# Layer 1's first norm with full-width column sums, and all residual transposes ahead of the expert-choice list

## The chip, the cores and the metric

The kernel runs on one core of a Trainium2 chip. The metric is the device time of one execution in microseconds (us); the result of several runs is given as a median. TensorE (PE) does matmuls and transposes, ScalarE (ACT) and VectorE (DVE) read PSUM and work on SBUF, GpSimd (POOL) issues indirect DMAs and does some elementwise work, SyncE (SP) issues the weight loads. Each engine runs its own instruction stream in order, and they meet at semaphores.

## The reference, cut to what matters

One inference step of a two-layer backbone over T = 640 tokens (512 sample tokens and 128 prompt tokens), width D = 1024. Each layer is a mixer and an expert-choice mixture of experts, each behind a root-mean-square norm and followed by a gated residual:

```python
def rms_norm(x, g):
    xf = x.astype(jnp.float32)
    y = xf * lax.rsqrt(jnp.mean(xf * xf, axis=-1, keepdims=True) + RMS_EPS)
    return (y * g.astype(jnp.float32)).astype(x.dtype)

def expert_choice_ffn(h, router_w, w1, w3, w2):
    ...
    aff = jax.nn.softmax(jnp.dot(xf, router_w).astype(jnp.float32), axis=-1)
    gate, idx = lax.top_k(aff.T, cap)          # 64 sample and 16 prompt tokens for each of 16 experts
    xe = xf[idx]
    hid = jax.nn.silu(jnp.einsum('ecd,edf->ecf', xe, w1)) * jnp.einsum('ecd,edf->ecf', xe, w3)
    ye = jnp.einsum('ecf,efd->ecd', hid, w2) * gate[..., None].astype(h.dtype)
    ...

def run_layer(x, mod, l, P, rope, ctx):
    h = rms_norm(x, P['norm1_g'][l]) * (1 + scale1) + shift1     # "first norm"
    y, new = even_mixer(...) if l % 2 == 0 else odd_mixer(...)
    x = x + gate1 * y
    h = rms_norm(x, P['norm2_g'][l]) * (1 + scale2) + shift2     # "second norm"
    x = x + gate2 * expert_choice_ffn(h, ...)
    return x, new
```

## The kernel before

Activations stand turned: `xT` and `hT` hold width in 8 blocks k of 128 partitions (KD = 8) and the 640 tokens along the free axis (`seg`: 512 sample, 128 prompt). A norm needs the sum over the width, so over partitions and over the 8 blocks, for each token. All data is fp32, and each fp32 matmul is two records in the profile, each transpose one.

**Layer 1's first norm** runs while layer 0's expert output is being added. `sum_pe` (L1565 to L1585) turns the expert output block by block (L1577, five 128x128 transposes for each k, into PSUM pairs 0, 1, 2 in turn); DVE adds the gated block to `xT` (L1189 for the 512 sample tokens, L1192 for the 128 others); ACT squares it into `sq_all` (L621); and PE, three blocks behind, sums the squares over partitions (L1583): here the squares are the stationary operand and one column of ones is the moving one, so each of five matmuls for each k gives 128 sums as one column, and `acc` in PSUM pair 3 ends as 128x5. Then ACT takes the root into `root5` (L625, 128x5), DVE the reciprocal (L646) and builds five diagonal blocks `diag5` from it (L647, 128x640), PE spreads these over all partitions with ones as the stationary operand (`norm_spread_pe`, L586 and L587), ACT copies the result to `rstd` (L357, a helper line), and DVE multiplies `xT` with it block by block (L663), ACT and DVE scale and shift the blocks (L632, L655), and the first projection of layer 1 takes each block as it comes (`proj_R_pe`, L702). `keep_busy` (L343) are matmuls whose result nobody reads; 12 stand at the head of `sum_pe`, two stand before L702.

**Expert choice in layer 1** (`route_pe`, `route_act`, `route_dve`): after the router's logits PE turns the normed rows (`hr`, five token tiles, L1238), ACT copies them out and POOL stores them to DRAM as `h_rows` (L1345), DVE makes the softmax, and PE turns the affinities (L1253). DVE then searches the list of picked tokens: eight rounds of max, index and replace over 512 columns and two over 128 (L1332 to L1334). Meanwhile PE turns the residual `xT` back into rows (`residual_rows`, units `xr`, L1261, eight transposes for each of five token tiles), which the end of the kernel adds to. Tiles 0, 1, 2 stand ahead of the wait for the list (semaphore `top`), then gate and index of the list are turned (unit `gi`, L1273 and L1274), then tiles 3 and 4. ACT copies each tile to `xrow`, which has the place of the rows stored by L1345, so ACT waits for that store (`h_stored`) first. `moe_pe` follows: three `keep_busy` matmuls, the transposes of expert 0's gathered rows (L1379), two groups of 16 matmuls that lay out the gates of the residual (`grow`, L1288), and then 16 experts, the first matmuls of which are L1396. The gather of expert 0's rows is an indirect DMA that POOL issues (L1481) once DVE has copied the turned index (L1340).

**What sets the order.** PSUM is used as four pairs of banks. `take(pe, name)` gives the next pair in rotation, or the one named, and PE waits until the last unit in that pair was released by its reader; `release` and `emptied` are the other side. Code order within each engine's function is the instruction order; there is no scheduler.

Of the kernel before, what the change touches and what calls it, by code (L numbers as in the profile page):

```python
# [18 lines left out]
ACT = mybir.ActivationFunctionType  # L19
# [3 lines left out]
P = 128  # L23
D = 1024
# [54 lines left out]
def build(nc, io, outs):  # L79
    with ExitStack() as ctx:  # L80
# [5 lines left out]
        def S(name):  # L86
            if name not in sems:
                sems[name] = ctx.enter_context(nc.semaphore("s_" + name))
            return sems[name]
# [88 lines left out]
        def filled(eng, name):  # L178
            pair, n = units.of[name]
            eng.wait_ge(pair_full[pair], n)  # L180
            return PSUM[:, pair, :]

        def release(ins, name):
            ins.then_inc(pair_free[units.of[name][0]], 1)

        def emptied(eng, name):
            pair, n = units.of[name]
            eng.wait_ge(pair_free[pair], n)
# [393 lines left out]
        def norm_spread_pe(pe, l, n):  # L582
            u = ("nrb", l, n)
            ps = take(pe, u)
            pe.wait_ge(S("n_diag"), 2 * l + n + 1)
            pe.matmul(ps[:, 0:NS], ones, diag5[:, 0:NS], start=True, stop=True)  # L586
            finish(pe.matmul(ps[:, NS:T], ones, diag5[:, NS:T], start=True, stop=True), u)  # L587

        def norm_spread_act(act, l, n):
            u = ("nrb", l, n)  # L590
            release(copy(act, rstd, filled(act, u)[:, 0:T]), u)
# [19 lines left out]
        def norm_squares_act(act, l, n):  # L611
# [3 lines left out]
            for k in range(KD):  # L615
# [4 lines left out]
                    act.wait_ge(S("sq_add"), ADDS[l, n] + max(1, k - 2))  # L620
                act.activation(sq_all[:, k, :] if (l, n) == (1, 0) else sq[:, k % 2, :], xT[:, k, :], ACT.Square).then_inc(S("sq"), 1)  # L621

        def norm_root_act(act, l, n):
            ps = filled(act, ("nrm", l, n))
            release(act.activation(root5, ps[:, 0:NT], ACT.Sqrt, scale=1.0 / D, bias=1e-6), ("nrm", l, n))  # L625

        def norm_shift_act(act, l, n):
# [15 lines left out]

        def norm_rstd_dve(v, step, l, n):
            emptied(v, ("nrm", l, n))
            step(v.reciprocal(root5, root5))  # L646
            v.tensor_tensor(diag5.rearrange("p (t c) -> p t c", c=P), ident.unsqueeze(1).broadcast_to((P, NT, P)),  # L647
                            root5.unsqueeze(2).broadcast_to((P, NT, P)), ALU.mult).then_inc(S("n_diag"), 1)

        def norm_scale_dve(v, l, n):  # L650
            def shifted(k):
                normed(v, l, n, k)
                for g in range(2):
                    a, b = seg[g]
                    ins = v.tensor_scalar(hT[:, k, a:b], hT[:, k, a:b], gsc[:, l, n, k, g:g + 1],  # L655
                                          modt[:, l, 24 * n + k, g:g + 1], ALU.mult, ALU.add)
                ins.then_inc(S("h_dve"), 1)

            for k in range(KD):
                emptied(v, x_unit(l, n, k))  # L660
            emptied(v, ("nrb", l, n))
            for k in range(KD):
                v.tensor_tensor(hT[:, k, :], xT[:, k, :], rstd, ALU.mult).then_inc(S("x_dve"), 1)  # L663
                if k in H_DVE:
                    shifted(k)
# [557 lines left out]
        def route_pe(pe, l):  # L1223
# [41 lines left out]
            if l == 1:  # L1265
                pe.wait_ge(S("x_half"), 24)
                for k in range(4, KD):
                    emptied(pe, ("out", 1, k))
                residual_rows((0, 1, 2))
            pe.wait_ge(S("top"), l + 1)  # L1270
            u = ("gi", l)
            ps = take(pe, u)
            pe.transpose(ps[0:CAP, 0:16], g16, ident[0:NE, 0:NE])  # L1273
            finish(pe.transpose(ps[0:CAP, 16:32], i16f, ident[0:NE, 0:NE]), u)  # L1274
            if l == 1:
                residual_rows((3, 4))

# [286 lines left out]
        def sum_pe(pe, l):  # L1566
            un = ("nrm", 1, 0)
            acc = take(pe, un, 3)
            keep_busy(pe, acc, 12)
            for k in range(KD + 3):  # L1570
                if k < KD:
                    if k % 2 == 0:
                        pe.wait_ge(S(f"m_quarter{k // 2}"), 16)
                    u = ("ms", l, k)
                    ps = take(pe, u, k % 3)
                    for t in range(NT):
                        last = pe.transpose(ps[:, t * P:t * P + P], rows_m[:, t, k * P:k * P + P], ident)  # L1577
                    finish(last, u)
                j = k - 3
                if j >= 0:  # L1580
                    pe.wait_ge(S("sq"), 16 + j + 1)
                    for t in range(NT):
                        last = pe.matmul(acc[:, t:t + 1], sq_all[:, j, t * P:t * P + P], ones[:, 0:1],  # L1583
                                         start=(j == t == 0), stop=(j == KD - 1 and t == NT - 1))
            finish(last, un)  # L1585


# [1016 lines left out]
        def _(pe):  # L2604
            setup_pe(pe)
            for l in range(2):
# [29 lines left out]
                moe_pe(pe, l)  # L2636
                if l == 0:
                    sum_pe(pe, l)
                    norm_spread_pe(pe, 1, 0)

        @block.scalar
        def _(act):
            step = Steps(act, S("act_step"))
            setup_act(act, step)
            for l in range(2):
# [3 lines left out]
                norm_root_act(act, l, 0)  # L2649
                if l == 0:  # L2650
                    mod_act(act, 2)
                norm_spread_act(act, l, 0)
                if l == 0:
                    mod_act(act, 3)
                norm_shift_act(act, l, 0)
                if l == 0:
# [158 lines left out]
```

## Time and profile before

| | us |
|---|---|
| median of 3 runs | 1795.73 |
| lowest and highest | 1794.01, 1798.09 |
| the profiled execution, its own time | 1794.16 |
| its span, first to last instruction | 1791.7 |
| PE busy | 1607.9 (90%) |
| DVE, ACT, POOL busy | 633.5, 439.5, 239.3 |
| granted TensorE clock, mean of the span | 0.953 |

A granted clock of 1.00 is 2.4 GHz, one of 0.50 is 1.2 GHz. A timeline row gives start, length, engine, line, what is written and read, the count, and in brackets the idle time of the engine before it with what ended it. PE is a matmul's stream and PEld a weight load, which overlaps it. The chain of waits is followed back from the last instruction: at each step to what released it.

### The profile page before, as it was taken

To read this page: it belongs to the slowest core of one execution; us is meant where nothing else is said; L and a number is where in the kernel's file an instruction comes from. 1 tells how busy PE (TensorE), PEld (TensorE's weight loads), DVE (VectorE), ACT (ScalarE), POOL (GpSimd) and SP (SyncE) were. 2 spreads that over 40 slices of the span, in tenths; PEclk is the share of its full clock that TensorE was granted. 3 is DMA by queue.
4 is the path that set the end of the run, shared out by engine and by line. 5 is a ranking of instruction groups with operands and counts; after the bars stand their busy time and mean duration, and the time that the engine had idled before them with its cause. 6 is when DMAs were issued, how large, how long until landed. Compare 5 with 4: busy or idle time off the path is not lost.

```text
span 1791.7 us, 37993 instructions
## 1 busy us (share of the span) xinstructions
PE 1607.9 (90%) x16758; PEld 1040.3 (58%) x16758; DVE 633.5 (35%) x1290; ACT 439.5 (25%) x734; POOL 239.3 (13%) x237
## 2 busy tenths in 40 slices
PE   5999976999959999999999989888899959999992
PEld 2554434664527677676555558666675536776761
DVE  4234466652260000003129646645462270000003
ACT  3211175551031111102110246432231031111110
POOL 0000000000001111100000026156440000111113
PEclk8999997999969999998999999999899979999996
DMA  9932281244218999994121100011115227999994
GB/s 341 307 115 94 100 288 46 95 142 188 94 74 307 385 382 394 380 379 143 47 71 71 50 1 1 1 50 50 49 50 200 73 85 247 372 388 387 386 394 142
DMA packets 90319, 330.09 MB, mean 184 GB/s; under 512 B 10708, under 2 KB 16456, under 8 KB 82024
## 3 DMA queue, kind: packets, MB, share of 16 engines
q1 hardware_dynamic: 76016, 287.29, 42.1%
q0 software_dynamic: 9168, 32.65, 6.6%
q10 hardware_dynamic: 5032, 8.65, 1.3%
q8 instruction: 80, 1.31, 0.3%
q14 instruction: 23, 0.19, 0.0%
HBM read 303.79 MB, written 24.78 MB: 183 GB/s over the span
## 4 chain that ended last, share of the span: by engine, by line
PE 83%; DVE 9%; ACT 3%; issue 2%; DMA 2%; POOL 0%; ACTq 0%; DVEq 0%
PE pairs L223 27%; PE pairs L1396 16%; PE pairs L1408 12%; PE pairs L1379 2%; PE pairs L343 2%; PE pairs L1096 2%; PE pairs L1110 1%; PE pairs L1886 1%; PE pairs L1866 1%; PE pairs L2093 1%; PE pairs L1849 1%; PE pairs L490 1%; PE pairs L461 1%; PE pairs L2104 1%; PE pairs L702 1%
## 5 line engine op out<-in xcount | busy, mean ns | idle before, releaser
L223 PE MATMUL pairs<-hT,ring 128*128 128x128 f32 (+1 forms) x1120 | 306.2, 436 | 2.2 <-ACT hT L357 2.2
L223 PEld LDWEIGHTS pairs<-hT,ring 128*128 128x128 f32 x1120 | 170.3, 192 | 139.0 <-issue 139.0
L357 ACT ACTIVATE arena<-pairs 128x512 f32<-128x512 f32 (+6 forms) x212 | 123.7, 602 | 430.3 <-PE pairs L223 198.8
L223 PE MATMUL pairs<-ring,hT 128*128 128x512 f32 (+1 forms) x448 | 177.4, 557 | 0.0
L1396 PEld LDWEIGHTS pairs<-arena,ring 128*64 128x64 f32 x4096 | 142.9, 137 | 13.6 <-issue 13.6
L1396 PEld LDWEIGHTS pairs<-arena 128*64 128x64 f32 x4096 | 142.8, 137 | 13.2 <-issue 13.1
L1396 PE MATMUL pairs<-arena 128*64 128x80 f32 x4096 | 145.5, 233 | 1.6 <-ACT arena L1431 1.0
L1396 PE MATMUL pairs<-arena,ring 128*64 128x80 f32 x4096 | 145.8, 233 | 0.5 <-issue 0.5
L223 PEld LDWEIGHTS pairs<-ring,hT 128*128 128x128 f32 x448 | 84.8, 190 | 92.1 <-issue 89.1
L1464 DVE TENSOR_SCALAR hT<-pairs,arena 80x512 f32<-80x512 f32 x32 | 23.9, 747 | 272.0 <-ACT hT L1440 272.0
L1408 PE MATMUL pairs<-ring,arena 128*80 128x512 f32 x256 | 112.7, 593 | 0.2 <-DMA ring<-in_exp_w 0.2
L1408 PE MATMUL pairs<-arena 128*80 128x512 f32 x256 | 112.5, 592 | 0.0
L1460 DVE TENSOR_TENSOR arena<-hT,pairs 128x160 f32<-128x160 f32 x64 | 20.5, 321 | 249.3 <-PE pairs L1396 249.3
L357 DVE COPY arena<-pairs 128x512 f32<-128x512 f32 (+7 forms) x37 | 25.2, 703 | 185.1 <-PE pairs L223 178.7
L1491 POOL DMA_INDIRECT moe_rows<-hT,arena x32 | 45.4, 1420 | 293.7 <-DVE hT L1464 293.7
L1408 PEld LDWEIGHTS pairs<-ring,arena 128*80 128x80 f32 x256 | 37.7, 152 | 63.1 <-issue 62.9
L1408 PEld LDWEIGHTS pairs<-arena 128*80 128x80 f32 x256 | 37.8, 153 | 62.6 <-issue 62.6
L1440 ACT ACTIVATE hT<-pairs,arena 80x512 f32<-80x512 f32 x32 | 21.9, 683 | 212.1 <-PE pairs L1408 212.1
L1431 ACT ACTIVATE arena<-pairs 128x640 f32<-128x640 f32 x32 | 22.5, 703 | 185.6 <-PE pairs L1379 185.6
L1189 DVE SCALAR_TENSOR_TENSOR xT<-pairs,modt,xT 128x512 f32<-128x512 f32 x24 | 18.0, 750 | 140.8 <-PE pairs L223 125.7
L343 PE MATMUL pairs<-cst 128*128 128x512 f32 x118 | 63.4, 680 | 3.8 <-ACT arena L357 2.1
L1481 POOL DMA_INDIRECT hT<-h_rows,arena x32 | 29.4, 917 | 241.3 <-PE pairs L1379 199.5
(393 smaller groups left out, 2139.6 us busy)
## 6 DMA issues: line engine op xcount, KB each, us to landing
arena<-in_exp_w SPq DMA_DIRECT2D x48, 2048.0 KB, 18.8
ring<-in_exp_w SPq DMA_DIRECT2D x48, 2048.0 KB, 20.1
ring<-in_w_mod SPq DMA_DIRECT2D x24, 2048.0 KB, 8.2
ring<-in_w_in_ab SPq DMA_DIRECT2D x5, 2048.0 KB, 11.9
ring<-in_w_in_cd SPq DMA_DIRECT2D x5, 2048.0 KB, 7.8
ring<-in_w_out SPq DMA_DIRECT2D x4, 2048.0 KB, 8.8
moe_rows<-arena POOLq DMA_DIRECT2D x2, 2560.0 KB, 12.8
h_rows<-arena POOLq DMA_DIRECT2D x2, 2560.0 KB, 8.2
```

Source lines behind the costliest of these rows:

```text
L223: last = pe.matmul(out, lhs(k), rhs(k), start=(k == 0), stop=(k == KD - 1))
L343: pe.matmul(ps[:, 0:512], ident, cst[:, 0:4, :].rearrange("p a b -> p (a b)"), start=True, stop=True)
L357: return eng.activation(dst, src, ACT.Copy) if eng is nc.scalar else eng.tensor_copy(dst, src)
L1096: pe.matmul(ps[:, 0:512], q, k[:, 0:512], start=True, stop=True)
L1379: last = pe.transpose(ps[:, o:o + CAP], xe[par][:, k::KD], ident[0:CAP, 0:CAP])
L1396: last = pe.matmul(lin_of(j, f)[c:c + 64, :], w[:, k, f * P + c:f * P + c + 64], rhs, start=(k == 0), stop=(k == KD - 1))
L1408: last = pe.matmul(PSUM[0:CAP, 3, 512 * half:512 * half + 512], hid[par][:, f, :], w2[:, f, 512 * half:512 * half + 512], start=(f == 0), ...
L1431: act.activation(xeT[par], ps, ACT.Copy).then_inc(pair_free[0], 1)
L1440: act.activation(ye[par][:, 0:512], PSUM[0:CAP, 3, 0:512], ACT.Copy, scale=gateT[:, bass.ds(i, 1)])\
L1464: v.tensor_scalar(ye[par][:, 512:1024], PSUM[0:CAP, 3, 512:1024], gateT[:, bass.ds(i, 1)], None, ALU.mult).then_inc(pair_free[3], 1)
L1481: g.indirect_dma_start(xe[e % 2], None, DR["h", l], off(e)).then_inc(S(f"gathered{e % 2}"), 16)
L1491: g.indirect_dma_start(DR["m", l], off(e), ye[e % 2], None, compute_op=ALU.add)\
```

## The change

Three things are edited.

1. In `sum_pe` the sums of layer 1's first norm take `ones` (128x128) as the stationary operand and the squares as the moving one, in two matmuls for each k (512 and 128 columns): each gives the sums of all its tokens on every partition, and `acc` is 128x640.
2. ACT takes the root over 128x640 from PSUM straight into `rstd`, DVE the reciprocal of it in place, and `diag5`, the two spreading matmuls, their PSUM unit (`nrb`) and ACT's copy go for this norm alone. The other three norms are as before; the counts of `n_diag` are renumbered.
3. In `route_pe` of layer 1 `residual_rows` for all five tiles stands ahead of the wait for `top`.

```diff
@@ norm_spread_pe
-            pe.wait_ge(S("n_diag"), 2 * l + n + 1)
+            pe.wait_ge(S("n_diag"), (1, 2, 0, 3)[2 * l + n])
@@ norm_root_act
             ps = filled(act, ("nrm", l, n))
+            if (l, n) == (1, 0):
+                release(act.activation(rstd, ps[:, 0:T], ACT.Sqrt, scale=1.0 / D, bias=1e-6), ("nrm", l, n))
+                return
@@ norm_rstd_dve
             emptied(v, ("nrm", l, n))
+            if (l, n) == (1, 0):
+                step(v.reciprocal(rstd, rstd))
+                return
@@ norm_scale_dve
-            emptied(v, ("nrb", l, n))
+            if (l, n) != (1, 0):
+                emptied(v, ("nrb", l, n))
@@ route_pe
-                residual_rows((0, 1, 2))
+                residual_rows(range(NT))
             pe.wait_ge(S("top"), l + 1)
             ...
-            if l == 1:
-                residual_rows((3, 4))
@@ sum_pe
-                    for t in range(NT):
-                        last = pe.matmul(acc[:, t:t + 1], sq_all[:, j, t * P:t * P + P], ones[:, 0:1],
-                                         start=(j == t == 0), stop=(j == KD - 1 and t == NT - 1))
+                    for a, b in seg:
+                        last = pe.matmul(acc[:, a:b], ones, sq_all[:, j, a:b], start=(j == 0), stop=(j == KD - 1))
@@ block.tensor
                     sum_pe(pe, l)
-                    norm_spread_pe(pe, 1, 0)
@@ block.scalar
-                norm_spread_act(act, l, 0)
                 if l == 0:
+                    norm_spread_act(act, l, 0)
                     mod_act(act, 3)
```

On PE, at the end of `sum_pe`, before (L1577 are the turned expert blocks, L1583 the sums, L586 and L587 the spreading, L702 the projection):

```order
L1577 MATMUL pairs<-cst,arena 128x128 x5
L1583 MATMUL pairs<-cst,arena 128x1 x20
L586 MATMUL pairs<-arena,cst 128x512
L587 MATMUL pairs<-arena,cst 128x128
L343 MATMUL pairs<-cst 128x512 x2
L702 MATMUL pairs<-ring,hT 128x512 x16
```

The same place after (all lines are some numbers on: L1583 are now the turned blocks, L1589 the sums, L710 the projection; the four pairs of L1589 are the last four blocks' sums):

```order
L1583 MATMUL pairs<-cst,arena 128x128 x5
L1589 MATMUL pairs<-arena,cst 128x512
L1589 MATMUL pairs<-arena,cst 128x128
L1589 MATMUL pairs<-arena,cst 128x512
L1589 MATMUL pairs<-arena,cst 128x128
L1589 MATMUL pairs<-arena,cst 128x512
L1589 MATMUL pairs<-arena,cst 128x128
L1589 MATMUL pairs<-arena,cst 128x512
L1589 MATMUL pairs<-arena,cst 128x128
L343 MATMUL pairs<-cst 128x512 x2
L710 MATMUL pairs<-ring,hT 128x512 x16
```

No PE instruction stands any more between the last sum and the two `keep_busy` matmuls.

On PE around the list of picked tokens in layer 1, with the semaphores that each instruction waits for, before (L1261 residual rows, L1273 and L1274 the turned list, L343 `keep_busy`, L1379 expert 0's rows):

```order
L1261 MATMUL pairs<-cst,xT 128x128 [waits s_pair_free1]
L1261 MATMUL pairs<-cst,xT 128x128 x7
L1273 MATMUL pairs<-cst,arena 80x16 [waits s_pair_free2,s_top]
L1274 MATMUL pairs<-cst,arena 80x16
L1261 MATMUL pairs<-cst,xT 128x128 [waits s_pair_free3]
L1261 MATMUL pairs<-cst,xT 128x128 x7
L1261 MATMUL pairs<-cst,xT 128x128 x7
L1261 MATMUL pairs<-cst,xT 128x128 [waits s_pair_free0]
L1261 MATMUL pairs<-cst,xT 128x128 x7
L343 MATMUL pairs<-cst 128x512 [waits s_pair_free3,s_pair_free0,s_pair_free2,s_pair_free1]
L343 MATMUL pairs<-cst 128x512 x2
L1379 MATMUL pairs<-cst,hT 128x80 [waits s_pair_free0,s_gathered0]
```

And after (L1269 residual rows, L1281 and L1282 the turned list, L1385 expert 0's rows):

```order
L1269 MATMUL pairs<-cst,xT 128x128 [waits s_pair_free1]
L1269 MATMUL pairs<-cst,xT 128x128 x7
L1269 MATMUL pairs<-cst,xT 128x128 [waits s_pair_free2]
L1269 MATMUL pairs<-cst,xT 128x128 x7
L1281 MATMUL pairs<-cst,arena 80x16 [waits s_pair_free3,s_top]
L1282 MATMUL pairs<-cst,arena 80x16
L343 MATMUL pairs<-cst 128x512 [waits s_pair_free0]
L343 MATMUL pairs<-cst 128x512 x2
L1385 MATMUL pairs<-cst,hT 128x80 [waits s_pair_free0,s_gathered0]
```

All 40 residual transposes stand ahead of the list's wait, and the pairs that these instructions take are one lower in the rotation, since the unit `nrb` is gone.

## Rows read from the trace of the kernel before

**Rows 1.** The page: the chain of waits by engine, shares of the span.
```profile
PE 83%; DVE 9%; ACT 3%; issue 2%; DMA 2%; POOL 0%; ACTq 0%; DVEq 0%
```
**Rows 2.** Chain of waits, 824 to 849 us: start, length, engine and line.
```profile
825.85 1.01 PE pairs L1583 x10
826.86 0.60 PE pairs L1577 x5
...
833.28 8.34 PE pairs L1583 x40
```
**Rows 3.** Windows of PE, 822 to 854 us: length, busy, granted clock, DMA, GB/s.
```profile
826.00:830.00 4.00, 4.00 (x39) 1.00 0.47 129
830.00:832.00 2.00, 2.00 (x17) 0.78 1.06 378
844.00:848.00 4.00, 4.00 (x8) 0.50 0.00 0
848.00:850.00 2.00, 2.00 (x6) 0.95 0.01 4
```
**Rows 4.** Chain of waits around 1441 us: matmuls of 512 and 128 moving columns.
```profile
1440.80 0.87 PE pairs L1231 x2
1441.67 0.22 PE pairs L1232 x2
```
**Rows 5.** Timeline, 841 to 849 us: from the last sum to the projection.
```profile
841.64 0.17 ACT L625 ACTIVATE sm<-pairs 128x5 f32<-128x5 f32 x1 [5.24 <-PE pairs L1583]
843.11 2.04 PE L586 MATMUL pairs<-arena,cst 128*128 128x512 f32 x2 [1.50 <-DVE arena L647]
845.62 0.70 ACT L357 ACTIVATE arena<-pairs 128x640 f32<-128x640 f32 x1 [3.80 <-PE pairs L587]
846.45 3.77 DVE L663 TENSOR_TENSOR hT<-xT,arena 128x640 f32<-128x640 f32 x5 [3.49 <-ACT arena L357]
848.57 3.70 PE L702 MATMUL pairs<-ring,hT 128*128 128x512 f32 x8
```
**Rows 6.** Groups by form on DVE: reciprocals by width, count, busy, mean ns.
```profile
L2388 DVE RECIPROCAL sm<-sm 128x40 f32<-128x40 f32 x1 | 0.4, 403 | 0.8 <-ACT sm L2268 0.8
L1055 DVE RECIPROCAL sm<-sm 128x16 f32<-128x16 f32 x1 | 0.2, 243 | 0.0
L646 DVE RECIPROCAL sm<-sm 128x5 f32<-128x5 f32 x4 | 0.8, 188 | 13.2 <-ACT sm L625 13.2
```
**Rows 7.** Windows of PE, 1452 to 1484 us: length, busy, granted clock, DMA, GB/s.
```profile
1456.00:1462.00 6.00, 0.00 (x0) 0.77 0.96 397
1483.00:1484.00 1.00, 1.00 (x4) 0.96 0.00 0
```
**Rows 8.** Timeline, 1462 to 1480 us: copies of residual rows, the list, the gather.
```profile
1462.20 2.86 ACT L357 ACTIVATE arena<-pairs 128x1024 f32<-128x1024 f32 x3 [8.83 <-DMA h_rows<-arena]
1474.44 0.24 PE L1273 MATMUL pairs<-cst,arena 16*80 16x16 f32 x1 [19.09 <-DVE arena L1336]
1475.45 0.98 POOL L1481 DMA_INDIRECT hT<-h_rows,arena  x1 [20.60 <-DVE arena L1340]
1479.56 4.55 PE L343 MATMUL pairs<-cst 128*128 128x512 f32 x6 [1.21 <-ACT arena L357]
```
**Rows 9.** Chain of waits, 1474 to 1498 us.
```profile
1474.75 3.62 PE pairs L1261 x16
...
1484.12 0.84 PE pairs L1379 x8
...
1488.58 9.00 PE pairs L1396 x256
```
**Rows 10.** One line's DMAs: issue to landing of gathers (L1481), then of stores (L1345).
```profile
DMA to landing us min/median/max: 3.8/3.9/4.0
DMA to landing us min/median/max: 8.2/8.2/8.2
```
**Rows 11.** What PE waited for, 1488 us to the end: in total, times, longest.
```profile
PE pairs L1408 <- DMA ring<-in_exp_w: 0.2, 1, 0.2
```

## The prediction

> **What bounds the kernel now.** I read the chain first, then the two places that the diff touches. The page gives 83% of the chain to PE [rows 1], so what shortens a stretch where the chain runs through PE or waits for it shortens the run. Both places are on that chain. At the first norm of layer 1 it runs through PE's turns of the expert output and the column sums, alternating [rows 2], then ACT, DVE, PE, ACT, DVE, ACT in turn, until the projection starts at 848.57 [rows 5]. At the expert choice it runs through DVE's search of the list, then the turned list on PE (1474.44) [rows 8], and from there only through PE: residual tiles 3 and 4, `keep_busy`, expert 0's rows, the gates, the experts [rows 9]. Behind both places PE sets the pace: in the whole stretch from 1488 us on it waited 0.2 us for anything but itself [rows 11], and the weight loads wait for PE's release of their slots, so they start earlier along with it. A gain at either place should reach the end whole.
>
> **The clock at the first norm is the thing to see.** The granted clock is 1.00 until about 830, while one-column sums and transposes are all that PE does, then it falls to 0.50 in the window 830 to 832 and comes back at about 848.2 (0.95 over 848 to 850) [rows 3]. So the last four blocks' sums ran at half speed: 8.34 us for four [rows 2], 2.09 each, against 1.01 for one at full clock.
>
> **Part 1a, the sums.** A full-width sum is one matmul of 512 and one of 128 moving columns. At clock 1.00 such matmuls took 0.87 and 0.22 [rows 4], 1.09 together, against 1.01 for five one-column ones [rows 2]: at equal clock the new form costs 8 x 0.08 = 0.6 us more. But PE streams columns nearly without a pause in it (1.09 of each 1.09 + 0.60), as it does in stretches where the clock stayed 1.00, where before 1.01 of 1.61 were weight loads with one column each. I take it that the clock stays at 1.00. From the first sum at 825.85 there are 8 x 1.09 + 4 x 0.60 = 11.1 us of work, ending at 836.97 instead of 833.28 + 8.34 = 841.62: **-4.65**. Nothing else is late there: the last block's transposes are done at 825.85 + 4 x 1.69 = 832.6, and its sum can't start before 835.9, which leaves 3.3 us for DVE's add and ACT's square of 640 elements, operations of a size that takes 0.70 to 0.75 [rows 5].
>
> **Part 1b, from the last sum to the blocks.** Before, 841.62 to 846.45, which is 4.83 us of root, reciprocal, diagonal, spreading and copy. After: a root over 128x640 out of PSUM, near the copy of the same size, 0.70 [rows 5], 0.1 for the hand-over, and a reciprocal of 640 elements. The trace has none wider than 40: 5 elements took 0.188, 16 took 0.243, 40 took 0.403 [rows 6]. The slope is 6.1 ns an element from 5 to 40 and 6.7 from 16 to 40, so 0.403 + 600 x 6.1 or 6.7 gives 4.1 to 4.4; I take 4.2. With 0.05 of hand-overs: 5.05, so **+0.2**. The wide reciprocal eats all that the removed steps give.
>
> **Part 1c, PE's idle time behind it.** PE now goes from the last sum into two `keep_busy` matmuls, 2 x 0.87 = 1.7 us, to 838.7, and then has nothing until the first block is scaled and shifted: 836.97 + 5.05 + 2.12 (846.45 to 848.57, rows 5) = 844.1. Before, spreading and `keep_busy` filled the time up to L702, and the clock was up as it began. In an idle stretch that began 19.09 us ahead of 1474.44, so at 1455.35 [rows 8], the clock fell at about 1459.2 (0.77 over 1456 to 1462) [rows 7], 3.9 us in. 5.4 us of idle time is longer, so I expect the projection to start at 0.50. It came back 5.1 us after work resumed at 843.11 [rows 3, 5] and 3.5 us after 1479.56 (0.96 over 1483 to 1484) [rows 7, 8]. Half of that is lost: 1.75 to 2.55, nothing if the clock doesn't fall; **+1.8**. The blocks themselves don't bound it: DVE gives one each 0.75, and ACT's part kept up with a PE at full clock before (8 records, two blocks, in 3.70) [rows 5].
>
> Sum of part 1: -4.65 + 0.2 + 1.8 = **-2.65**.
>
> **Part 2, the residual tiles.** Tiles 3 and 4 leave the chain: 3.62 from 1474.75, and 1.2 of waiting for ACT to copy them ahead of `keep_busy` at 1479.56 [rows 8, 9]. Now `keep_busy` starts at 1474.75. It is still at half clock, since PE had been idle: 3 matmuls x 2 x 0.87 = 5.2 us, where before they took 4.55 because the clock came back within them. That ends at 1479.95. Expert 0's rows then have to be there: the gather was issued at 1475.45 and gathers landed in 3.8 to 4.0 [rows 8, 10], 1479.35, so hidden by 0.6. L1379 starts at 1479.95 instead of 1484.12: **-4.2**. It and the gates take 1488.58 - 1484.12 = 4.46, as before, if the clock is back by then, 5.2 us after work resumed. Bounds: -4.8, where the gather is the limit; -3.3, if the clock is 1.7 us late. The moved instructions are free where they go: PE was idle for 19 us. One new wait comes with it: tile 4 takes the pair of tile 0, which ACT copies only once the store of `h_rows` has landed, and the turned list is queued behind tile 4 on PE. ACT's copies began at 1462.20 [rows 8], so tile 4 is turned by about 1464.5, some 10 us before the list. ACT copies five tiles in place of three inside DVE's search and has nothing to do there.
>
> The rotation is one pair off through layer 1. The reuse distance stays four, and I cost it at nothing, within 0.5 either way.
>
> **The sum:** -2.65 - 4.2 = -6.85 against the profiled execution's 1794.16, giving 1787.3. That execution lies 1.57 under the median of the three; against the median it is 1795.73 - 6.85 = **1788.9**.
>
> **A rule that would make it otherwise.** Were the reciprocal eight passes over its elements, it would cost eight times a plain 128x640 multiply (3.77 for five, 0.754 each, rows 5): 6.0 us, so +1.8 on the sum, 1790.7. The 40-element row is 0.403 where eight passes at 0.754/640 an element would make 0.377 and leave next to nothing fixed, while the 5-element row shows some 0.15 fixed. So the trace leans to the slope, yet doesn't exclude it. The Trainium skill, in "VectorE: DVE Perf Modes", section "First, the fixed hardware budget", says that the reciprocal is an iterated divide with a repeat count of 8.
>
> **The rivals.** (A) The clock falls in the sums all the same, as before. Part 1a is then nothing, the sum is +0.2 + 1.8 - 4.2 = -2.2: 1793.5. For it: transposes are 0.60 of each round and were in the stretch that lost the clock. Against: the column sums now stream. (B) Eight passes, 1790.7, as above. (C) The clock survives the idle time: -8.65, 1787.1. Against it is the fall after 3.9 us. (D) Slower: PE is stuck in tile 4. The list is turned only after the store of `h_rows` has landed and two tiles are copied. The price is one us for each us that the store lands after about 1472; from 1472 + 6.85 = 1479 on, 17 us later than here, the kernel is slower than before, and at 1484 the time is 1800.7. The store landed at 1462.2. Part 2 then only trades its gain away. (E) The change does nothing on the chain, because something late elsewhere holds the end: 1795.7; rows 11 speak against it.
>
> **How the numbers follow.** Forecast 0.55, A 0.15, B 0.15, C 0.08, D 0.03, E 0.04. A change of 0.2% is 3.6 us, about what a measurement can tell from none: under 1792.1 is faster. The forecast, B and C are, but for some scatter (three runs of before span 4.1 us): 0.77. A and E are within 0.2%, with that scatter 0.19; slower 0.04. The range reaches from C with the best bound of part 2 (1786) less 0.5, to A: 1785.5 to 1793.5.
>
> **What would show it.** In the profile after: granted clock 1.00 through the sums, last sum about 4.7 us earlier (part 1a); one reciprocal of 4.1 to 4.4 us (1b; 6.0 would be B); PE idle for some 5.4 us ahead of the projection and 0.50 in its first 3 to 5 us (1c); no PE record between the turned list and `keep_busy`, and expert 0's rows about 5.2 us after the list, not 9.4 (part 2). Wrong would be: the clock down in the sums, a gather that lands after `keep_busy`, or PE waiting for weights among the experts.

## The result, and the profile after

| | before | after |
|---|---|---|
| median, us | 1796.72 (4 runs, 1794.01 to 1798.09) | 1784.80 (4 runs, 1783.37 to 1789.75) |
| ratio after / before | | 0.994, 95% interval 0.9916 to 0.9964 |
| the profiled execution, its own time | 1794.16 | 1789.75 |
| its span | 1791.7 | 1787.8 |

The kernel is faster, by 11.9 us in the medians. I had predicted 6.85 us. The predicted ratio, 1788.9 / 1795.73 = 0.9962, lies in the interval of the measured one, near its slow end. The predicted range ended at 1785.5, and the median is 0.7 us below it. A second series of the same kernel (e1 below) gave 1785.14, ratio 0.9937. So the direction was right and the size was too small. The profiled execution of after was the slowest of its four, and that of before was quicker than most of its kind. The two traces show 3.9 us of difference between them; the medians show three times that.

The page of after, with busy times by engine and the chain by engine (of before: rows 1):

```profile
span 1787.8 us, 37877 instructions
PE 1604.2 (90%) x16706; PEld 1031.6 (58%) x16706; DVE 637.9 (36%) x1289; ACT 439.7 (25%) x733; POOL 239.1 (13%) x237
PE 83%; DVE 10%; ACT 3%; DMA 2%; issue 2%; POOL 0%; ACTq 0%; DVEq 0%
```

PE is still 83% of the chain. DVE's rounded share reads 10% instead of 9%; the 4.16 us of the reciprocal are now on the chain in one piece.

**Part 1, the norm.** PE in windows from 830 to 854 us: length, busy, granted clock, DMA share, GB/s. In rows 3 the clock of before is 0.78 in the first of these.

```profile
830.00:832.00 2.00, 2.00 (x13) 1.00 0.46 71
832.00:836.00 4.00, 4.00 (x21) 1.00 1.07 393
836.00:840.00 4.00, 4.00 (x15) 1.00 1.02 375
840.00:844.00 4.00, 0.30 (x1) 1.00 0.03 7
844.00:848.00 4.00, 2.28 (x3) 0.55 0.00 0
...
850.00:854.00 4.00, 4.00 (x9) 0.85 0.00 0
```

The chain of waits of after in this stretch: start, length, engine and line. L1583 are the turned blocks, L1589 the wide sums, L627 the root, L651 the reciprocal, L671 and L636 scale a block, L710 is the projection (of before: rows 2).

```profile
827.75 1.08 PE pairs L1589 x4
828.83 0.55 PE pairs L1583 x5
...
834.26 4.34 PE pairs L1589 x16
...
838.62 0.71 ACT arena L627
...
839.43 4.16 DVE arena L651
...
843.61 0.83 DVE hT L671
...
844.47 1.21 ACT hT L636 x2
...
845.72 16.72 PE pairs L710 x32
```

The timeline of after at its two important rows (of before: rows 5):

```profile
839.43 4.15 DVE L651 RECIPROCAL arena<-arena 128x640 f32<-128x640 f32 x1 [4.12 <-ACT arena L627]
845.72 4.63 PE L710 MATMUL pairs<-ring,hT 128*128 128x512 f32 x5 [5.42 <-ACT hT L636]
```

The clock stays at 1.00, which is 2.4 GHz, through all sums, and the last four blocks take 4.34 us where they took 8.34. One round is 1.08 + 0.55. The reciprocal is 4.15 us. PE is idle for 5.42 us ahead of the projection. The clock goes to 0.50 (1.2 GHz) in the window 844 to 848, shortly before the idle time ends, and comes back in the window 850 to 854. So the projection's 32 records take 16.72 us; before they took 13.91, with the clock up.

**Part 2, the list.** The chain of after from the turned list (L1281) to the experts (L1402), and two timeline rows: ACT's copies of the five residual tiles, PE's turns of the last one, and the wait of expert 0's rows for their gather (of before: rows 8 and 9).

```profile
1474.74 0.24 PE pairs L1281
...
1475.05 4.89 PE pairs L343 x6
1479.94 0.97 PE pairs L1385 x8
1480.91 3.61 PE pairs L1294 x32
1484.53 9.00 PE pairs L1402 x256
```

```profile
1462.51 4.69 ACT L357 ACTIVATE arena<-pairs 128x1024 f32<-128x1024 f32 x5 [8.83 <-DMA h_rows<-arena]
1463.58 1.97 PE L1269 MATMUL pairs<-cst,xT 128*128 128x128 f32 x8 [7.06 <-ACT arena L357]
1479.80 0.30 PEld L1385 LDWEIGHTS pairs<-cst,hT 80*128 80x128 f32 x2 [0.90 <-DMA hT<-h_rows,arena]
```

From the turned list to the experts' first matmul it is 1484.53 - 1474.74 = 9.8 us; before it was 1488.58 - 1474.44 = 14.1. The last tile is turned by 1465.5, some 9 us before the list. The gather is only just hidden: the weight load at 1479.80 had waited for it.

### The profile page after: what moved, and what is told of

It reads as the page before. It is cut to its first block, busy times and chain, and to the rows that moved or that the text cites. A ratio compares the mean times of both kernels' runs of the same rounds, so it can differ in the third digit from the quotient of the medians.

```text
span 1787.8 us, 37877 instructions
## 1 busy us (share of the span) xinstructions
PE 1604.2 (90%) x16706; PEld 1031.6 (58%) x16706; DVE 637.9 (36%) x1289; ACT 439.7 (25%) x733; POOL 239.1 (13%) x237
## 3 DMA queue, kind: packets, MB, share of 16 engines
q10 hardware_dynamic: 5032, 8.65, 1.3%
## 4 chain that ended last, share of the span: by engine, by line
PE 83%; DVE 10%; ACT 3%; DMA 2%; issue 2%; POOL 0%; ACTq 0%; DVEq 0%
PE pairs L223 27%; PE pairs L1402 16%; PE pairs L1414 12%; PE pairs L1385 2%; PE pairs L1104 2%; PE pairs L343 1%; PE pairs L1118 1%; PE pairs L1871 1%; PE pairs L1891 1%; PE pairs L2098 1%; PE pairs L1854 1%; PE pairs L710 1%; PE pairs L490 1%; PE pairs L461 1%; PE pairs L2109 1%
## 5 line engine op out<-in xcount | busy, mean ns | idle before, releaser
L1402 PEld LDWEIGHTS pairs<-arena,ring 128*64 128x64 f32 x4096 | 142.8, 137 | 14.5 <-issue 14.5
L1402 PEld LDWEIGHTS pairs<-arena 128*64 128x64 f32 x4096 | 142.7, 137 | 13.1 <-issue 13.0
L1402 PE MATMUL pairs<-arena,ring 128*64 128x80 f32 x4096 | 145.7, 233 | 1.5 <-issue 1.5
L1402 PE MATMUL pairs<-arena 128*64 128x80 f32 x4096 | 145.4, 233 | 1.5 <-ACT arena L1437 1.0
L1414 PEld LDWEIGHTS pairs<-ring,arena 128*80 128x80 f32 x256 | 37.7, 152 | 62.8 <-issue 62.6
L343 PE MATMUL pairs<-cst 128*128 128x512 f32 x118 | 60.8, 656 | 2.6 <-DVE hT L1470 1.7
```

Source lines behind the costliest of these rows:

```text
L343: pe.matmul(ps[:, 0:512], ident, cst[:, 0:4, :].rearrange("p a b -> p (a b)"), start=True, stop=True)
L1402: last = pe.matmul(lin_of(j, f)[c:c + 64, :], w[:, k, f * P + c:f * P + c + 64], rhs, start=(k == 0), stop=(k == KD - 1))
L1414: last = pe.matmul(PSUM[0:CAP, 3, 512 * half:512 * half + 512], hid[par][:, f, :], w2[:, f, 512 * half:512 * half + 512], start=(f == 0), ...
```

## Experiments

What had to be explained was that the medians differ by more than the two traces. The suspects were: the clock in the sums (my theory), the pair rotation, one part hiding more than its trace showed, and the profile of before being an unusual one. Kernels that were measured together share their runs of before: median 1795.57 for e1 to e4 and 1796.31 for e5 to e8 (17 runs each), 1796.0 for e9 to e12 (11 runs). The three groups ran on different chips, so a kernel of one group is compared with one of another by its ratio to before. A bracket behind a ratio is its 95% interval.

### e1: the changed kernel again

> The changed kernel as it is, with more runs on one chip together with its two halves. Theory 1 (the sum of the prediction): about 6.4 to 6.9 us under the kernel before, and the 11.9 us between the two medians of four runs is partly scatter. Theory 2 (something outside the two places gives 4 to 5 us more, for example the PSUM pairs that are one lower through all of layer 1): 10 to 12 us under it again.

1785.14 us (5 runs, 1782.79 to 1787.32), ratio 0.9937 [0.9922, 0.9953]. The gain is 10.4 us in the medians. The larger value was no accident of the first series.

### e2: the norm alone

```diff
-                residual_rows(range(NT))
+                residual_rows((0, 1, 2))
             pe.wait_ge(S("top"), l + 1)
             ...
+            if l == 1:
+                residual_rows((3, 4))
```

> Only the norm's part of the change (wide sums, root and reciprocal; the shifted pairs come with it), residual tiles 3 and 4 behind the list as before. Theory 1: -2.0 to -2.7 us: the sums end 4.7 us earlier for the clock, the wide root and reciprocal give back 0.2, the projection's start at 1.2 GHz 1.8 to 2.8. Theory 2: -6 to -8 us, since the shifted pairs belong to this half. In its profile expert 0's first matmuls stand about 14 us behind the turned list, as in the kernel before.

1785.61 us (5 runs), ratio 0.9947 [0.9931, 0.9962]: the norm alone is worth 10.0 us in the medians, 9.5 by the ratio. I had given it 2.65, and neither theory had as much. Its trace also shows what the residual tiles cost in that state. The chain from the first of tiles 3 and 4 (L1269) on:

```profile
1468.49 3.60 PE pairs L1269 x16
1472.10 3.27 PE pairs L343 x6
1475.36 0.84 PE pairs L1387 x8
```

The `keep_busy` matmuls took 3.27 us, where before they took 4.55, since the clock came back within them (0.66 in the window 1472 to 1474). And they did not have to wait for ACT's copy of tile 4, which starts only as they do:

```profile
1472.13 1.02 ACT L357 ACTIVATE arena<-pairs 128x1024 f32<-128x1024 f32 x1 [0.68 <-PE pairs L1269]
```

That is the pair rotation at work. In before tile 4 takes pair 0, the one that `keep_busy` needs next; one pair lower it takes pair 3. From list to experts it is 11.6 us here, against 14.1 in before with the same order of code: 1.3 us of the difference are the clock, 1.2 the wait for the copy. Against the mean of three executions of before, this one is 3.5 us shorter at the norm and its records, 2.9 from the list on, and 5.4 between DeltaNet and the second norm, which the edit doesn't touch (table below).

### e3: the residual tiles alone

The edits of the norm undone, that of `residual_rows` kept.

> Only the residual tiles moved ahead of the list's wait, the norm as before. Theory 1: -4.2 us (bounds -3.3 to -4.8), all of it between the turned list and expert 0's first matmuls: 9.6 us there in place of 14.1, and nothing elsewhere. Theory 2: also about -4. If the two halves add up to e1, nothing lies in their combination.

1792.95 us (11 runs, 1790.56 to 1795.56), ratio 0.9986 [0.9975, 0.9996]: 2.6 us in the medians, where I had predicted 4.2. Its chain behind the list:

```profile
1480.04 5.41 PE pairs L343 x6
1485.45 0.84 PE pairs L1377 x8
...
1489.91 6.09 PE pairs L1394 x171
```

From the list at 1479.17 to the experts it is 10.7 us in this execution. `keep_busy` begins 0.87 us behind the list, and not 0.31 as in after: with the old rotation the turned list lies in pair 0, and DVE has to copy it out first. The 10.7 us are 3.4 to 3.9 less than the 14.1, 14.2 and 14.6 of three profiles of before, and the upper end of the median's gain (0.9975, 4.5 us) holds it. The two parts together (2.6 + 10.0) are 12.6, the whole 10.4 to 11.9: they add up within the intervals.

### e4: eight `keep_busy` matmuls in PE's idle time

```diff
-                    keep_busy(pe, ps, 2)
+                    keep_busy(pe, ps, 8)
```

> The changed kernel with 8 instead of 2 of the matmuls that nobody reads ahead of layer 1's first projection: 7.0 us at full clock from the last sum on, which ends about when the first block is there (7.2 us). Theory 1: the clock stays at 2.4 GHz into the projection, whose first 32 records take 13.9 us instead of 16.7, so -1.8 to -2.8 us against the changed kernel. A rival (the loss lies in the first blocks' arrival, not in the clock): no change, and the same 16.7 us.

1783.66 us (6 runs, 1780.14 to 1788.3), ratio 0.9931 [0.9913, 0.995]. PE in the window behind the reciprocal, and the chain at the projection:

```profile
844.00:848.00 4.00, 3.73 (x10) 1.00 0.00 0
```

```profile
845.13 14.00 PE pairs L710 x32
```

With PE occupied, the clock stays at 1.00 and the 32 records take 14.00 us, as in before. So the idle time, and nothing else in the change, was what made them 16.7 and 16.0 (after and e1). That settles part 1c: its cost is 2.0 to 2.8 us. In the medians e4 is 1.5 us under e1, inside the intervals.

### e5: the pair rotation as before

```diff
                     sum_pe(pe, l)
+                    units.next += 1
```

> The changed kernel with the rotation of the PSUM pairs moved on by one behind the column sums, so that every later unit of layer 1 has the pair that it had in the kernel before. The norm alone gave 9.5 us in medians where its place in the traces gives 2 to 5. Theory 2 (the pairs, one lower, give the rest): 4 to 6 us slower than the changed kernel. Theory 1 and theory 3 (the old form costs more than the one profile shows, because how early the clock falls in it is a matter of luck): no change against it, about 0.9937 of the kernel before.

1788.27 us (6 runs, 1781.5 to 1790.94), ratio 0.9944 [0.9921, 0.9966]. With the rotation of before and the rest of the change, the gain stands. Theory 2 had this kernel 4 to 6 us slower than the changed one. By the ratios it is 1.3 us slower than e1, and its interval reaches 4 us to each side, so the medians alone would allow the rotation a share. The trace shows one effect of it (list at 1473.87):

```profile
1474.73 4.88 PE pairs L343 x6
```

`keep_busy` starts 0.86 us behind the list where after has 0.31, as in e3. So the lower rotation is worth some 0.55 us in the changed kernel. No stretch of e5's trace is longer than in both traces of the changed kernel by more than 0.9 us (table below).

### e6 and e11: the old sums with wide matmuls between them

Before, with one 128x512 matmul that nobody reads behind each of the first seven blocks' sums (e6), and with two (e11). The sums themselves remain 128x5.

```diff
                         last = pe.matmul(acc[:, t:t + 1], sq_all[:, j, t * P:t * P + P], ones[:, 0:1],
                                          start=(j == t == 0), stop=(j == KD - 1 and t == NT - 1))
+                    if j < KD - 1:
+                        keep_busy(pe, acc[:, 512:1024], 1)      # 2 in e11
```

> The kernel before (one-column sums, narrow root and reciprocal, spreading) with one 128x512 matmul that nobody reads behind each of the first seven blocks' sums: 6.1 us more work for PE at 2.4 GHz, in the stretch that sets the time. Theory 1 (a PE that streams no columns loses the clock): the clock stays at 2.4 GHz until the sums end, the spreading is at full clock too, and the projection starts 24.5 to 25.5 us after the first turned block, against 25.7 in the profile of the kernel before and 28.0 in that of the run with the tiles alone: 0 to -3 us. Theory 3: -2 us or more, since the unlucky cases go. If columns had nothing to do with the clock: +6 to +12 us.

1799.04 us (12 runs, 1793.47 to 1806.41), ratio 1.0018 [1.0001, 1.0035]. This expectation missed: the kernel is some 3 us slower than before and not up to 3 us faster, and the clock fell ahead of the end of the sums. The profiled execution is the second slowest of the twelve (1806.34 us).

> e6 with two unread 128x512 matmuls behind each of seven blocks' sums instead of one: 12.2 us more work for PE than the kernel before. In e6 the clock lasted until about 841, 10 to 13 us longer than without, and then fell with one matmul for each five one-column sums. Theory 1 (streamed columns hold the clock): 1.00 until the last sum at about 849, so that from the first turned block to the projection's start there are 30 to 31.5 us. If the one-column sums are what drops it whatever stands between them: a fall ahead of 845 and 35 us or more.

1795.97 us (one run). In the chain of e6 the sums are 1.01 us until 840 and 1.92 after it; the window is below them:

```profile
839.39 1.01 PE pairs L1583 x10
840.40 1.86 PE pairs L343 x2
842.26 1.92 PE pairs L1583 x10
```

```profile
840.00:844.00 4.00, 4.00 (x16) 0.54 0.01 5
```

In e11 the last sum is at full clock too:

```profile
849.27 1.02 PE pairs L1583 x10
```

So what PE does between the one-column sums decides when the clock falls: at 828 to 832 with none (four executions), at 840 with one wide matmul to each block, and not within the sums with two (one execution each). All three stretches have PE busy throughout. That is what the change rests on, shown without the change. The extra work costs more than it gives: from the first turned block to the projection e6 takes 30.7 us and e11 32.1, before 25.7 to 28.0, after 20.9. Replacing narrow sums by wide ones gives the columns for nothing.

### e7 and e10: the kernel before, profiled again

> The kernel before, profiled once more. Theory 3: the stretch from the first turned block to the end of the first projection's 32 records differs from that of the first profile (39.7 us) and is nearer to that of the run with the tiles alone (42.0) or over it; with the new form it was 37.0 to 37.6 three times. Theory 1 without luck: 39.7 again, within 0.3.

1797.43 us (one run, span 1795.5).

> The kernel before, profiled a third time. If the norm's stretch is mostly the longer one: from the first turned block to the projection's start 28.0 us again, not 25.7, and a fall of the clock near 1128 us, between the grouped attention and DeltaNet, as in all three profiles with narrow sums so far and in none with wide ones.

1798.32 us (one run, span 1795.8). In e7 the fall comes three us earlier than in rows 3. Its windows and its chain:

```profile
826.00:830.00 4.00, 4.00 (x30) 0.75 0.50 142
830.00:832.00 2.00, 2.00 (x12) 0.50 1.08 391
```

```profile
827.83 0.90 PE pairs L1577 x5
828.73 1.92 PE pairs L1583 x10
```

Two more rounds run at 1.2 GHz. From the first turned block to the projection it is 28.0 us here and in e3, 25.7 and 25.8 in before and e10. So theory 3 had e7 right, and the expectation of e10 missed: the longer stretch is not the usual one. Its second part, a fall of the clock near 1128 us, held. The profile that I predicted from was one of the quicker kind: against a mean of 26.5 over the three executions of before, it made this stretch 0.8 us too short.

### e9: the projection later, with the clock up

Ten `keep_busy` matmuls in e4's place of eight.

> e4 with 10 in place of 8 unread matmuls ahead of the projection: at full clock everything behind it comes 1.5 us later (8.7 us of work in a 7.2 us gap), and nothing else changes. What is open is why the kernels with narrow sums took 282 to 288 us in layer 1's second half (from DeltaNet's first transposes to the second norm's root) where those with wide sums took 279 to 282.5. Theory 3 (when the later stages come, not what they do, sets how often the clock falls in them): the medians differ by something other than 1.5 us, and the profile has other falls of the clock than e4 behind 1040 us. Theory 4 (the later stages don't depend on it): +1.5 us against e4, that is 0.994 of the kernel before.

1784.96 us (6 runs, 1782.11 to 1789.95), ratio 0.9948 [0.9931, 0.9964]. The stretch up to the projection is 22.2 us where e4 has 20.9: +1.3. The medians differ by the same 1.3, the ratios by 3 us, each uncertain by as much. In the profiled execution, though, the later stages were 4 us shorter than in e4's (278.5 against 282.5 from DeltaNet to the second norm). So a shift of 1.3 us can go with another pattern of falls later. The medians don't show it as a rule.

### e8 and e12: the gates' rows ahead of the list as well

e4, and besides in layer 1 the gates' 16 matmuls (`grow`) stand ahead of the list's wait. In e8 five `keep_busy` matmuls stand behind the list, in e12 three. ACT's copies of the gates' rows move ahead along with them. (The 16 matmuls are two groups of eight, each group 16 records.)

```diff
                 residual_rows(range(NT))
+                gate_rows_pe(pe)
             pe.wait_ge(S("top"), l + 1)
...
-            keep_busy(pe, PSUM[:, 0, :], 3)
+            keep_busy(pe, PSUM[:, 0, :], 5 if l else 3)
```

> The changed kernel with 8 matmuls ahead of the projection as in e4, and the 32 gate records (L1294) turned ahead of the list too, while DVE searches it, with 5 instead of 3 of the unread matmuls behind the list in layer 1. Expected: expert 0's rows at the gather's landing, some 4.9 us after the turned list as before, its first matmuls 6.5 to 7 us after the list in place of 9.7; -3 us against e4, -4.5 to -5.5 against the changed kernel. A rival: the clock is down again behind the list (PE was waiting), and half of the gain goes.

1782.42 us (6 runs, 1778.49 to 1786.01), ratio 0.992 [0.99, 0.9941].

> e8 with 3 instead of 5 unread matmuls behind the list. In e8 the clock was at 1.2 GHz behind the list, the five took 7.6 us and held expert 0's rows until 1475.0 where the gather had landed at about 1472. Expected: 5.2 us at half clock, so the rows at 5.2 us and the first expert matmuls at 7.1 us behind the list in place of 9.6; -2.4 us against e8 for that. A rival: the experts' first matmuls then run at half clock for some us and the gain halves.

1784.32 us (6 runs, 1778.64 to 1790.51), ratio 0.9938 [0.9917, 0.9958]. The chain of e8 and then of e12 behind the list:

```profile
1467.45 7.55 PE pairs L343 x10
1474.99 0.86 PE pairs L1387 x8
...
1476.81 9.07 PE pairs L1404 x256
```

```profile
1472.08 4.02 DMA hT<-h_rows,arena
...
1476.14 1.13 PE pairs L1387 x8
...
1478.23 10.71 PE pairs L1404 x256
```

In e8 the five `keep_busy` matmuls ran mostly at half clock and took 7.55 us. From list to experts it is 9.7 us, no better than the 9.8 of after, where 6.5 to 7 had been expected; the rival of that expectation, a clock that is down behind the list, is what came. In e12 it is 7.1 us, as expected, and the gather now sets it (4.02 us on the chain). But the experts' first 256 records take 10.71 us instead of 9.00, with the clock at 0.50 in this window:

```profile
1480.00:1482.00 2.00, 2.00 (x35) 0.50 0.26 88
```

One more such trade: here work taken off PE ahead of the experts was paid in clock within them, and instead of 2.4 us less the median is 1.9 us more than e8's. e8 has the lowest median of all. Its interval overlaps those of e4 and e12, so what is shown is that e8 beats before, not that it beats e4 or the changed kernel. The gates' move has no gain of its own that these runs show.

## Why the prediction was right, and too small

The table shows the stretches of all fourteen profiled executions in us, each cut at the same instructions: first turned block of the expert output, first projection matmul, last of its 32 records, first transposes of DeltaNet, root of the second norm, turned list of layer 1. The last column is the span. Before, e7 and e10 are the same kernel, and so are after and e1.

| | to first block | to projection | its 32 records | to DeltaNet | to second norm | to list | to end | span |
|---|---|---|---|---|---|---|---|---|
| before | 822.9 | 25.7 | 14.0 | 288.4 | 282.0 | 41.4 | 317.3 | 1791.7 |
| e7 | 822.2 | 28.0 | 14.0 | 287.2 | 285.3 | 41.3 | 317.5 | 1795.5 |
| e10 | 823.7 | 25.8 | 14.0 | 288.4 | 284.9 | 40.9 | 318.1 | 1795.8 |
| e3, tiles | 824.1 | 28.0 | 14.0 | 287.2 | 284.9 | 41.0 | 313.0 | 1792.2 |
| e2, norm | 823.7 | 21.0 | 16.0 | 287.5 | 278.7 | 41.3 | 314.7 | 1782.9 |
| after | 824.8 | 20.9 | 16.7 | 288.4 | 282.4 | 41.5 | 313.1 | 1787.8 |
| e1, after | 824.0 | 20.9 | 16.0 | 287.6 | 282.1 | 41.2 | 313.6 | 1785.4 |
| e4 | 824.2 | 20.9 | 14.0 | 287.5 | 282.5 | 41.7 | 313.2 | 1784.0 |
| e9 | 824.3 | 22.2 | 14.0 | 286.9 | 278.5 | 41.4 | 312.8 | 1780.1 |
| e8 | 825.1 | 20.9 | 14.0 | 286.2 | 280.3 | 40.6 | 312.6 | 1779.7 |
| e12 | 824.3 | 21.0 | 14.0 | 287.5 | 282.6 | 41.7 | 312.6 | 1783.7 |
| e5 | 825.0 | 21.0 | 16.4 | 289.3 | 280.8 | 41.4 | 313.7 | 1787.6 |
| e6 | 824.3 | 30.7 | 14.0 | 289.3 | 287.9 | 41.9 | 315.9 | 1804.0 |
| e11 | 824.3 | 32.1 | 13.9 | 288.5 | 278.3 | 40.8 | 316.1 | 1794.0 |

**Part 1a, the sums: right, and 0.25 us larger.** Clock 1.00 throughout. From the first sum to the last it is 838.60 - 827.75 = 10.85 us, predicted 11.1, since a round was 1.63 and not 1.69. Before it was 15.77. So 4.9 us instead of 4.65 against that profile, and 0.8 us more against the mean of before's three. Rival A is out: in all eight executions with wide sums the clock stayed at 1.00 until the last of them, though the transposes, 0.55 of each 1.63 us, are still there. e6 and e11 point the same way. Whether the transposes had a share in the fall before, beside the one-column sums, these runs don't separate.

**Part 1b, root and reciprocal: right.** 838.60 to 843.61 is 5.01 us, predicted 5.05. The reciprocal took 4.15 us; the slope of its narrow forms had given 4.1 to 4.4, with 4.2 taken. Rival B, eight passes or 6.0 us, is out. The Trainium skill ("VectorE: DVE Perf Modes", section "First, the fixed hardware budget") gives the reciprocal a repeat count of 8. The measured 4.15 us is 5.5 times the 0.754 of a plain multiply of this size, so the repeat count can't be read as eight times the time.

**Part 1c, the idle time: right in kind, too small.** 5.42 us idle, predicted 5.4, and the projection starts at 0.50. The 32 records cost 2.8 us more in after and 2.0 in e1, predicted 1.8 with bounds of 1.75 to 2.55. That half of the time until the clock is back is lost was right: in after it was back at 851.2 (0.89 in the window 851 to 852), 5.5 us after the projection began, for a cost of 2.8, and in e1 at 849.0, 4.1 us after, for 2.0. What was mis-sized is that time. The prediction had 3.5 to 5.1 us and took +1.8, nearly the low end, without a reason. And the 3.5 was read too short: it counts from 1479.56, but PE had been at work on the list and tiles 3 and 4 from 1474.44 to 1478.35, so the clock came back 8.6 us after work had resumed there. The fall comes earlier in e1, too, 2.7 us into the idle time (839.5 to 844.9) where after has 4.1. Its windows at the fall and at the return:

```profile
842.00:844.00 2.00, 0.00 (x0) 0.55 0.00 0
...
849.00:850.00 1.00, 1.00 (x3) 0.99 0.00 0
```

Rival C, a clock that survives, is out; e4 shows what it would have been worth.

**Part 2, the residual tiles: right in this trace.** List to experts 14.1 to 9.8 us, 4.3, predicted 4.2. Expert 0's rows start 5.2 us after the list, as predicted. The gather was hidden by 0.1 us or less and not 0.6: it was issued at 1475.75, and PE's weight load had it at 1479.80. Rival D is out: tile 4 was turned 9 us before the list. What I had not seen is that this term hangs on the clock. With tiles 3 and 4 behind the list the same stretch is 14.1, 14.2 and 14.6 us in the executions of before, but 12.4 in e6 and 12.0 in e11, whose code is that of before from there on and where the clock came back sooner, and 11.6 in e2, where the rotation helps as well. With them ahead it is 9.7 to 10.7. So how much the edit saves differs with the clock, from 4.3 us to some 2 (an estimate from 11.6 to 12.4 less 9.7 to 10.7), which fits the 2.6 us of e3's medians.

**The pair rotation at nothing, within 0.5: just about right for the whole change**, where it gives 0.55 us at the list, by e5 and e3. For the norm alone it is not nothing: 1.2 us of e2's gain are the wait for ACT's copy that it removes.

**What was missing.** Taken from executions instead of one, the two places give: up to the projection 26.5 to 20.9 (-5.6), its records 14.0 to 16.35 (+2.35), list to end 317.6 to 313.35 (-4.3), each as the mean of before, e7 and e10 and of after and e1. That is -7.5 us, where I had -6.85. The medians say 10.4 to 11.9. So one weak step is the one that made one execution stand for the kernel, "-6.85 against the profiled execution's 1794.16". Mended, it gives 0.7 of the missing 3.6 to 5 us. Some 3 to 4 us remain that neither place holds. In the medians the two halves were off in opposite directions, 10.0 where I had 2.65 and 2.6 where I had 4.2, so the whole came nearer than its larger part: that much is luck. The range has a slip of its own. Rival C with the best bound of part 2 is 1795.73 - 8.65 - 0.6 = 1786.5, not 1786, and the low end would have been 1786.0.

The traces themselves leave almost nothing open: the mean spans of the three and the two executions, 1794.3 and 1786.6, differ by 7.7 us. But both traced executions of the changed kernel are the slowest of their series (1789.75 of four, 1787.32 of five), and over all runs the means differ by 10.5 us (1795.8 over 45 runs of before in the experiments, 1785.3 over nine of after). What is missing lies mostly in executions without a trace.

I looked for it in the stages in between, which the change doesn't touch. From the end of the projection's records to the second norm's root, the four executions with old sums and no wide matmuls between them take 570.4 to 573.3 us, mean 572.1, and the eight with wide sums 565.4 to 570.8, mean 568.6. That would be 3.5 us. An example is PE's clock from 1120 to 1160, first in before and then in after:

```profile
1120.00:1160.00 40.00, 36.24 (x344) 0.96 0.01 1
```

```profile
1120.00:1160.00 40.00, 35.78 (x366) 1.00 0.00 1
```

That looks like a system, but e11, with old sums, has 0.96 in the same window and yet 566.8 us in the stretch, e6 has 577.2, and after and e1 alone are only 1.8 us under the three of before. It is a hint and not more.

Every run also records its mean granted clock, which is a wider sample than fourteen traces. Over 45 runs of before it is 0.9534, over nine of after 0.9581. The time at half clock, 2 x (1 - clock) x span, is 167.3 and 149.4 us as the mean of the runs: 17.9 us less, uncertain by about 6, since one run scatters by 8. By the same formula for a stretch and its granted clock, and as the same means as above, it is 18.2 to 6.8 us up to the end of the projection's records. From the list on it has to be read in narrow windows, since 0.01 of the clock over 317 us is 6 us. The difference is here, first in before and then in after:

```profile
1480.00:1486.00 6.00, 6.00 (x25) 0.74 0.02 5
```

```profile
1480.00:1486.00 6.00, 6.00 (x84) 1.00 0.27 79
```

So read, it is 37.7 to 33.5 us. The two places together are 15.6 us less, and 2 us, give or take 6, are left for the stages in between: neither shown nor excluded. The remaining 3 to 4 us are open. The interval of e1's ratio allows a gain of 8.4 to 14.0 us, and the 7.5 us found are 0.9 under its lower end, while the first series allows 6.5 to 15.1. So part of the rest may be scatter; which part, these runs don't tell.

## What to carry to other kernels

Sums with one moving column look as cheap as wide ones, but here eight rounds of them and transposes, with PE busy all the time, lost the clock: 17 to 21 us at half speed up to the projection. Where the wide form costs 0.07 us a round more at equal clock, take it, and then look at what the shorter stretch leaves idle behind it, because PE's next work pays for that (2.0 to 2.8 us here, and nothing with six more matmuls in the gap). A unit less in a rotation of buffers moves all later ones, and can remove or add a wait far away (0.55 and 1.2 us here): look at which unit each wait then names. Whoever predicts a few tenths of a per cent should take three profiles of the kernel before, and see where each lies among the runs without one: here one stretch was 25.7 or 28.0 us, the same code, as the clock fell one or two rounds earlier.

## What the runs showed of the hardware

- A busy PE is not enough to keep 2.4 GHz. In before PE is busy without a pause from 826 on and the clock falls at 831 (0.78 in the window 830 to 832), and in e7 at 828; with one 128x512 matmul to five one-column ones (e6) it falls at 840; with two (e11), not at all within the sums.
- A reciprocal of 640 fp32 elements on each of 128 partitions takes 4.15 us, and from 40 elements (0.403) to 640 it is (4.15 - 0.403) / 600 = 6.2 ns for each, close to the 6.1 from 5 to 40.
- In after the granted clock was still 1.00 some four us into an idle stretch (840 to 844), and came back 5.5 us after work had resumed. In e1 the same code lost it 2.7 us in and had it back after 4.1 us: the place varies from execution to execution by more than what many edits are worth.
- Work taken from PE just ahead of a busy stretch can be paid back in it: e12 saved 2.7 us ahead of the experts and lost 1.7 in their first 256 records.
